# Row-vector broadcasts over 128 rows instead of 4, and the last modulation groups dealt between the late mixer steps

## Chip, core and metric

One Trainium2 chip, one core. The metric is the device time in microseconds of one execution of the whole program: 1726.24 us is the median of 3 runs of the kernel before (1725.05 to 1731.7).

## What is computed

One inference step of a recurrent decoder, two layers, all in fp32, on a prompt of 256 tokens and 8 sampled sequences of 8 tokens (320 token columns together). Cut to what matters here:

```python
mods = (silu(c) @ ada_w + ada_b).reshape(B, 3, 3, 1, D_MODEL)     # shift, scale, gate of three sublayers
x = residual(x, 0, swiglu(modulate(x, 0), ...), 0.5)
proj = modulate(x, 1) @ w_in
o_rw  = rwkv7_mix(p_rw, ...)      # 6 heads of 64
o_gla = gla_mix(p_gla, ...)       # 4 heads, keys of 48, values of 96
o_ml  = mlstm_mix(p_ml, ...)      # 4 heads of 64
mix = concatenate([o_rw, o_gla, o_ml]) @ w_out
x = residual(x, 1, mix, 1.0)
x = residual(x, 2, swiglu(modulate(x, 2), ...), 0.5)
```

Inside the mLSTM, three quantities are one number per head and token (a row vector of 320 elements for each of 4 heads): a weight of the carried state `w_inter`, the argument `b - m_t` of the decay matrix `Dw = exp(D - m_t)`, and `exp(-m_t)`, the floor of the denominator. Each must be spread over the 64 rows of its head before VectorE can multiply with it.

## The kernel before

The core works with the model dimension on the partitions and the 320 token columns along the free side. A weight tile of 128 x 1024 fp32 is loaded, split by ScalarE and VectorE into a high and a low part (`whi`, `wlo`), and each product takes three matmuls (lines 2017 to 2019). The order of all work is fixed ahead: `PLAN` is a list of steps, and the program of every engine walks through the same list, so each engine has its own piece of a step in the same place. Engines wait for each other through semaphores.

In each layer the plan is: up and down projections of the first feed-forward; the input projection; the three mixers; the output projection; the second feed-forward. The mixers are generators (`rw_pe`, `gl_pe`, `ml_pe` for TensorE, with ones for the other engines), and a step "rw", "gl" or "ml" runs one of them to its next `yield`:

- A first part, spread by `layer_plan`, in which the RWKV steps invert triangular matrices: batches of 64x64 matmuls (line 784), each followed by VectorE operations on their results (lines 1157 to 1172) that the next batch reads. I call it the inverse.
- A second part, whose order is the string `LATE` (line 99): the late steps. They hold the state recurrence of RWKV (lines 851 to 872, 900, 902), attention of GLA (1272, 1281, 1294, then 1315 to 1326 and the norm's 1334), and the mLSTM: `ml_pe` turns rows into columns (1535), spreads the row `E2` over both head pairs (1540, "pairsel"), for each of three token tiles spreads `ER` (1546, "headsel"), multiplies keys by queries (1555) and transposes (1562), builds the states (1573), spreads `D1` (1578), and then multiplies (1596, 1603, 1608); 1615 and 1620 are the norm. At the end the sampled states are advanced (1812, 914, 1821) and the first tiles of the output projection follow ("hi", "lo", "early").

`con("pairsel", P, rows=4, ...)` means that the weights of the spreading matmul are 4 rows by 128 columns, and the row vectors, tiles `IG` (also `E2`), `ER` and `D1`, have 4 partitions. They lie over the memory of `XH` and `XL`, the split inputs of the products. ScalarE zeroes rows 64 to 127 of the GLA part of `XH` and `XL` for the output projection (line 1368); that is one of its GLA steps.

The modulations `mods` are the filler. One group of them is four chunks: `ada` (line 2032) multiplies a 128 x 1024 tile of `ada_w` as the moving side, in four places of 32 output rows of a PSUM bank, `psC` or `psY`. The trace shows a chunk as 8 matmuls of 256 columns. After the fourth chunk ScalarE copies the bank to `MR` (line 2247, "mrow_done"), and a step `fold` (line 2042) on TensorE, which waits for that copy, turns it, and VectorE adds it to `MODS` (line 2344). `in_tail` lists the groups that are dealt into the inverse: 7 of them in layer 0 and 3 in layer 1. Their chunks are loaded through the ring `raw` of four buffers. The late steps hold no chunk.

The code that the change touches, with the line numbers of the profile:

## Time and profile before

| | us |
|---|---|
| median of 3 runs | 1726.24 |
| lowest and highest run | 1725.05, 1731.7 |
| the profiled execution | 1723.39 |
| its span, first to last instruction | 1721.4 |
| TensorE busy in it | 1645.3 (96%) |
| VectorE, ScalarE, GpSimd busy | 945.6, 663.3, 179.3 |
| mean granted clock of TensorE | 0.942 of full |

The profile is of one execution. "Busy" is the union of the intervals in which the engine has an instruction in it. PEclk is the share of its full clock that TensorE was granted: 1.00 is 2.4 GHz and 0.50 is 1.2 GHz. A line "L784 PE MATMUL psV<-Yb,Tt 64*64 64x64 f32 x24" is 24 matmuls of source line 784, whose weights are 64 rows by 64 columns and whose moving side is 64 rows of 64 columns. Bracketed at the end stands the idle time of the engine before the row and what ended it.

### The profile page before, as it was taken

The page shows a single profiled execution, that of the slowest core. Times are in us where ns is not written, and L with a number is a line of the kernel's source. Part 1 is how long each engine was busy: PE and PEld are TensorE (multiplying, and loading weights), DVE is VectorE, ACT ScalarE, POOL GpSimd, SP SyncE. Part 2 cuts the span into 40 slices and gives each one's busy share as a digit, 9 for nine tenths or more (in the row PEclk, how much of TensorE's full clock was granted, in tenths as well). Part 3 has the DMA queues.
Part 4 walks back from the last instruction along what each step waited for, and adds up shares of the span by engine and source line. Part 5 has one row for each costly group of instructions (what it writes and reads, how often), then busy time and mean ns, then how long its engine had stood idle before and what let it go on. Part 6 is the DMA issues. An engine that isn't in the chain of part 4 may idle for free.

```text
span 1721.4 us, 32986 instructions
## 1 busy us (share of the span) xinstructions
PE 1645.3 (96%) x14132; PEld 1517.5 (88%) x14132; DVE 945.6 (55%) x1605; ACT 663.3 (39%) x959; POOL 179.3 (10%) x247
## 2 busy tenths in 40 slices
PE   5999999999999999999999999999898999999997
PEld 2999998978778779999989999989877877899996
DVE  1544546584643776555474454467755457755544
ACT  2333334463323445333354333355432133543333
POOL 1000012100202140000110000110020123100011
PEclk9999999999975899999999999999997559999999
DMA  8765465433631174444765545643422104544441
GB/s 308 269 229 213 157 230 176 163 104 123 209 118 41 48 266 135 148 147 150 253 208 190 192 148 191 222 168 110 135 87 57 40 14 160 202 151 154 149 147 67
DMA packets 92512, 270.22 MB, mean 157 GB/s; under 512 B 27184, under 2 KB 29648, under 8 KB 92112
## 3 DMA queue, kind: packets, MB, share of 16 engines
q1 hardware_dynamic: 87952, 265.50, 45.0%
q10 hardware_dynamic: 4416, 2.62, 0.6%
q8 instruction: 112, 1.84, 0.5%
q14 instruction: 32, 0.26, 0.1%
HBM read 261.83 MB, written 6.26 MB: 156 GB/s over the span
## 4 chain that ended last, share of the span: by engine, by line
PE 82%; DVE 11%; DMA 3%; ACT 2%; issue 1%; SPq 0%; POOL 0%; DVEq 0%; ACTq 0%; POOLq 0%
PE psV L2017 12%; PE psV L2018 12%; PE psV L2019 12%; PE psA L2017 9%; PE psA L2019 9%; PE psA L2018 9%; PE psV L784 3%; DMA raw<-weights_dram 3%; DVE wlo L2335 2%; PE psY L2032 1%; PE psC L2032 1%; DVE PJ L1504 1%; PE psV L1608 1%; PE psV L773 1%; PE psV L2042 1%
## 5 line engine op out<-in xcount | busy, mean ns | idle before, releaser
L2335 DVE TENSOR_TENSOR wlo<-raw,whi 128x1024 fp32r<-128x1024 f32 x334 | 412.7, 1238 | 399.8 <-ACT whi L2193 397.2
L2193 ACT ACTIVATE whi<-raw 128x1024 fp32r<-128x1024 f32 x334 | 352.3, 1056 | 327.8 <-PE psV L2019 303.9
L2017 PE MATMUL psA<-XH,whi 128*128 128x320 f32 x1120 | 350.3, 313 | 12.1 <-DVE wlo L2335 10.4
L2018 PE MATMUL psA<-XL,whi 128*128 128x320 f32 x1120 | 347.6, 310 | 0.0
L2019 PE MATMUL psA<-XH,wlo 128*128 128x320 f32 x1120 | 347.4, 310 | 0.0
L2017 PE MATMUL psV<-XH,whi 128*128 128x320 f32 x848 | 267.1, 315 | 0.2
L2018 PE MATMUL psV<-XL,whi 128*128 128x320 f32 x848 | 264.1, 311 | 0.0
L2019 PE MATMUL psV<-XH,wlo 128*128 128x320 f32 x848 | 263.9, 311 | 0.0
L2017 PEld LDWEIGHTS psA<-XH,whi 128*128 128x128 f32 x1120 | 211.8, 189 | 16.1 <-issue 13.2
L2017 PE MATMUL psV<-HH,whi 128*128 128x320 f32 x704 | 217.5, 309 | 0.0
L2019 PE MATMUL psV<-HH,wlo 128*128 128x320 f32 x704 | 217.5, 309 | 0.0
L2018 PE MATMUL psV<-HL,whi 128*128 128x320 f32 x704 | 217.5, 309 | 0.0
L2018 PEld LDWEIGHTS psA<-XL,whi 128*128 128x128 f32 x1120 | 211.9, 189 | 0.3
L2019 PEld LDWEIGHTS psA<-XH,wlo 128*128 128x128 f32 x1120 | 211.8, 189 | 0.0
L2017 PEld LDWEIGHTS psV<-XH,whi 128*128 128x128 f32 x848 | 161.4, 190 | 7.3 <-issue 5.7
L2018 PEld LDWEIGHTS psV<-XL,whi 128*128 128x128 f32 x848 | 161.2, 190 | 0.6 <-issue 0.4
L2019 PEld LDWEIGHTS psV<-XH,wlo 128*128 128x128 f32 x848 | 161.1, 190 | 0.0
L2017 PEld LDWEIGHTS psV<-HH,whi 128*128 128x128 f32 x704 | 132.2, 188 | 0.0
L2018 PEld LDWEIGHTS psV<-HL,whi 128*128 128x128 f32 x704 | 132.2, 188 | 0.0
L2019 PEld LDWEIGHTS psV<-HH,wlo 128*128 128x128 f32 x704 | 132.2, 188 | 0.0
L2291 ACT ACTIVATE SG<-psA 128x320 f32<-128x320 f32 x84 | 36.7, 437 | 197.6 <-PE psA L2019 197.6
L2468 DVE TENSOR_TENSOR HF<-SG,psV 128x320 f32<-128x320 f32 x84 | 40.9, 487 | 91.8 <-PE psV L2019 91.8
(401 smaller groups left out, 1928.6 us busy)
## 6 DMA issues: line engine op xcount, KB each, us to landing
raw<-weights_dram SPq DMA_DIRECT2D x408, 512.0 KB, 3.3
own<-weights_dram SPq DMA_DIRECT2D x56, 512.0 KB, 6.1
in_xh<-weights_dram SPq DMA_DIRECT2D x6, 512.0 KB, 4.6
in_xl<-weights_dram SPq DMA_DIRECT2D x6, 512.0 KB, 4.7
raw<-weights_dram SPq DMA_DIRECT2D x8, 256.0 KB, 3.7
in_hl<-weights_dram SPq DMA_DIRECT2D x4, 512.0 KB, 5.4
ZS<-st_rw_dram SPq DMA_DIRECT2D x2, 768.0 KB, 4.3
S<-st_gla_dram ACTq DMA_DIRECT2D x2, 768.0 KB, 4.9
```

Of the source, the lines that this page charges most:

```text
L773: ins = mm(bank[c, o:o + 128].rearrange("p (x t) -> p x t", x=2), lhs[p, j, tc:tc + CH], AR[p, :, j, tc:tc + CH], start=True, stop=True)
L784: ins = mm(bank[c, h * CH:(h + 1) * CH], lhs, rhs, start=True, stop=True)
L1504: V.do(stt(out, x(tap), pcol("conv_w", 4 * tap + i), out, ALU.mult, ALU.add))
L1608: ins = mm(bank[p, SEQ + DS * s:SEQ + DS * (s + 1)], C0[p, j, s, part], QW[p, j, SEQ + DS * s:SEQ + DS * (s + 1)], start=False, stop=True, ...
L2017: mm(out, split_hi(n)[:, k], hi[:, kt], start=first, stop=False)
L2018: mm(out, split_hi(n)[:, k], lo[:, kt], start=False, stop=False)
L2019: return mm(out, split_lo(n)[:, k], hi[:, kt], start=False, stop=last)
L2032: ins = mm(psM[BANK[group]][o:o + 32, 0:256], CT[:, 2 * q + k], w[:, k, half], start=(q == 0), stop=(q == 3))
L2193: activation(split_hi(n), buffer(DENSE[n]), ACT.Copy).then_inc(hi_done, 1)
L2291: A.do(activation(SG[:, u % 2], bank[:, 0:TOK], ACT.Silu), sem("gate_done"))
L2335: tt(split_lo(n), buffer(DENSE[n]), split_hi(n).bitcast(F32), ALU.subtract).then_inc(lo_done, 1)
L2468: V.do(tt(HF[:, u % 2], SG[:, u % 2], bank[:, 0:TOK], ALU.mult), sem("hidden_done"))
```

## The change

Three edits that go together:

1. The spreading matmuls take all 128 rows of the constant (zeros in the rows from 4 on) and of the row tiles, which are now `[128, 320]`. Rows 4 to 127 of the tiles are zeroed first: one memset of `IG_all` on VectorE ahead of the mLSTM's first operations, and two, `ER_all` and `D1_all`, on GpSimd ahead of its mLSTM rows.
2. Since the tall tiles lie over the rows of `XH` and `XL` that ScalarE zeroes, that zeroing moves from the GLA step to the mLSTM step behind the last spreading.
3. The last 3 groups of `in_tail` in layer 0 and the last 2 in layer 1 (`IN_LATE`) leave the inverse. `LATE` has new places "ada" (both layers), "ada_" (layer 0 alone) and "fold" (layer 0 alone; other folds follow their chunk). Layer 0 gets 12 chunks in its late steps, layer 1 gets 8. All groups dealt late use the bank `psC`.

```diff
+LATE = ("rw ml ada gl rw ml ada gl ml ada_ rw gl ml ada rw gl ml ada ada_ gl ada rw ml ada_ gl ada rw ml ada gl ada_ ml ada rw fold "
+        "gl rw ml su mix rs rw rs su hi.0 rs lo.0 rw hi.1 rw hi.2 lo.1 early.0 rw lo.2 early.1 rw").split()
+IN_LATE = (3, 2)
...
-    out += spread([(step, 1) for step in together], ada_groups(in_tail))
+    out += spread([(step, 1) for step in together], ada_groups(in_tail[:-IN_LATE[L]]))
+    chunks = ada_groups(in_tail[-IN_LATE[L]:])
...
+        out.append(chunks.pop(0))
+        while chunks and chunks[0][0] == "fold":
+            out.append(chunks.pop(0))
...
-        BANK[_step[1:4]] = _b = GROUPS.index(_step[1:4]) % 2
+        BANK[_step[1:4]] = _b = 0 if _step[1:4] in LATE_GROUPS else GROUPS.index(_step[1:4]) % 2
...
+        IG_all, ER_all, D1_all = (over(f"row{i}_all", [P, TOK], at) for i, at in ((0, xh[3]), (4, xl[3]), (7, xl[6])))
+        IG, ER, D1 = IG_all[0:MH], ER_all[0:MH], D1_all[0:MH]
...
-                for x in (XH, XL):
-                    A.do(activation(x[64:P, RP:RP + GH], CON[64:P, 0:GH * TOK].rearrange("p (h t) -> p h t", t=TOK), ACT.Copy, scale=0.0))
-                A.mark(sem("gl_zero"))
...
-                    bV.close(mm(bank[:, 0:TOK], con("pairsel", P, rows=4, at=j * P), E2[:], start=True, stop=True))
+                    bV.close(mm(bank[:, 0:TOK], con("pairsel", P, at=j * P), IG_all[:], start=True, stop=True))
...
-                            ins = mm(bank[c, h * CH:(h + 1) * CH], con("headsel", CH, rows=4, at=h * CH), ER[:, tc:tc + CH],
+                            ins = mm(bank[c, h * CH:(h + 1) * CH], con("headsel", CH, at=h * CH), ER_all[:, tc:tc + CH],
...
-                    bA.close(mm(bank[:, 0:TOK], con("pairsel", P, rows=4, at=j * P), D1[:], start=True, stop=True))
+                    bA.close(mm(bank[:, 0:TOK], con("pairsel", P, at=j * P), D1_all[:], start=True, stop=True))
...
+                V.do(nc.vector.memset(IG_all[:], 0.0))
...
+                G.do(nc.gpsimd.memset(ER_all[:], 0.0))
+                G.do(nc.gpsimd.memset(D1_all[:], 0.0))
```

How the instructions move, at three places. The names: `psC<-raw,CT` and `psY<-raw,CT` are chunks (x4 here is one chunk, which the trace shows as 8), `psV<-FOLD,MR` a fold, `row_...,CON` a spreading.

TensorE in the inverse of layer 0, from the middle of a batch on, before:

```order
L784 MATMUL psV<-Tt_153,Yb_116 64x64 x6
L2032 MATMUL psC<-raw,CT 32x256 x4
L784 MATMUL psV<-Tn_111,AM_102 64x64 x12
L784 MATMUL psV<-Tn_112,AM_104 64x64 x12
L2032 MATMUL psY<-raw,CT 32x256 x8
L1264 MATMUL psA<-CON,PJ 128x128 x6
L1264 MATMUL psA<-CON,PJ 64x128 x3
L2042 MATMUL psV<-FOLD,MR 128x18 x2
L784 MATMUL psV<-Yb_114,Tt_151 64x64 x12
```

and with the change:

```order
L800 MATMUL psV<-Tt_153,Yb_116 64x64 x6
L2054 MATMUL psY<-raw,CT 32x256 x4
L800 MATMUL psV<-Tn_111,AM_102 64x64 x12
L800 MATMUL psV<-Tn_112,AM_104 64x64 x12
L2064 MATMUL psV<-FOLD,MR 128x18 x2
L1280 MATMUL psA<-CON,PJ 128x128 x6
L1280 MATMUL psA<-CON,PJ 64x128 x3
L2054 MATMUL psY<-raw,CT 32x256 x4
L800 MATMUL psV<-Yb_114,Tt_151 64x64 x12
```

Between the same batches stand fewer chunks: 16 in the whole part in place of 28.

TensorE at the first spreadings of the late steps of layer 0, before:

```order
L1540 MATMUL psV<-row_166,CON 128x320 x2
L1272 MATMUL psA<-CON,PJ 128x128 x2
L1281 MATMUL psV<-PJ,GB 64x64 x8
L868 MATMUL psV<-U_122,TK_101 64x64 x6
L872 MATMUL psV<-TK_101 64x64 x6
L1546 MATMUL psV<-row_170,CON 64x64 x8
L1555 MATMUL psV<-PJ 64x64 x8
L1562 MATMUL psV<-CON,PJ 128x128 x2
L1272 MATMUL psA<-CON,PJ 128x128 x2
```

and with the change:

```order
L1553 MATMUL psV<-row_all,CON 128x320 x2
L2054 MATMUL psC<-raw,CT 32x256 x4
L1288 MATMUL psA<-CON,PJ 128x128 x2
L1297 MATMUL psV<-PJ,GB 64x64 x8
L884 MATMUL psV<-U_122,TK_101 64x64 x6
L888 MATMUL psV<-TK_101 64x64 x6
L1559 MATMUL psV<-row_all,CON 64x64 x8
L1568 MATMUL psV<-PJ 64x64 x8
L1575 MATMUL psV<-CON,PJ 128x128 x2
L2054 MATMUL psC<-raw,CT 32x256 x4
L1288 MATMUL psA<-CON,PJ 128x128 x2
```

A chunk now follows the first spreading and each token tile. In the later steps one follows each GLA product (1326) and, in layer 0, each mLSTM product (1608).

TensorE at the norms, near the end of the late steps of layer 0, before:

```order
L1334 MATMUL psV<-PJ,CON 96x320 x4
L1615 MATMUL psV<-PJ,CON 128x320 x2
L868 MATMUL psV<-U_123,TK_103 64x64 x6
L872 MATMUL psV<-TK_103 64x64 x6
L851 MATMUL psV<-Z,WT_149 64x64 x6
```

with the change:

```order
L1350 MATMUL psV<-PJ,CON 96x320 x4
L2054 MATMUL psC<-raw,CT 32x256 x4
L1628 MATMUL psV<-PJ,CON 128x320 x2
L2054 MATMUL psC<-raw,CT 32x256 x4
L2064 MATMUL psV<-FOLD,MR 128x18 x2
L884 MATMUL psV<-U_123,TK_103 64x64 x6
L888 MATMUL psV<-TK_103 64x64 x6
```

and ScalarE at the same place, with the change:

```order
L1399 ACTIVATE PJ<-PJ 96x1280
L1676 ACTIVATE PJ<-PJ 128x640
L2269 ACTIVATE MR<-psC 128x256
L1680 ACTIVATE PJ<-psV,EPS 128x320 x2
```

The last fold of the layer follows its own last chunk at once, and the copy to `MR` for which it waits stands in ScalarE's row behind the square of the mLSTM's output (line 1660 before, 1676 now).

## Rows read from the trace of the kernel before

**Rows 1.** The page: span, TensorE's share, and its granted clock in 40 slices

```profile
span 1721.4 us, 32986 instructions
...
PE 1645.3 (96%) x14132; PEld 1517.5 (88%) x14132; DVE 945.6 (55%) x1605; ACT 663.3 (39%) x959; POOL 179.3 (10%) x247
...
PEclk9999999999975899999999999999997559999999
```

**Rows 2.** Windows in us: length, busy time (instructions) of each engine, granted clock, DMA

```profile
445.00:483.70 38.70, 38.45 (x953) 32.42 (x953) 26.79 (x55) 10.34 (x19) 6.88 (x14) 1.00 0.64 215
501.60:522.00 20.40, 20.02 (x249) 16.42 (x244) 10.33 (x34) 4.43 (x7) 0.00 (x0) 0.50 0.15 32
...
525.50:559.60 34.10, 33.63 (x451) 30.40 (x448) 10.48 (x17) 9.19 (x14) 11.19 (x7) 0.50 0.07 29
...
1272.80:1311.20 38.40, 36.14 (x866) 32.03 (x865) 28.08 (x53) 9.88 (x16) 7.60 (x15) 0.91 0.24 80
1313.90:1324.20 10.30, 10.16 (x161) 8.85 (x157) 0.00 (x0) 5.45 (x13) 0.00 (x0) 0.50 0.01 2
...
1327.60:1351.00 23.40, 22.95 (x270) 18.50 (x270) 11.73 (x39) 4.82 (x8) 0.00 (x0) 0.50 0.17 45
1351.00:1392.40 41.40, 40.26 (x472) 34.34 (x472) 13.07 (x25) 13.19 (x18) 12.47 (x8) 0.50 0.11 40
```

**Rows 3.** Timeline, TensorE: start, length, what (rows*columns of the weights, moving side)

```profile
499.09 1.32 PE L1540 MATMUL psV<-row,CON 4*128 4x320 f32 x4
...
502.85 1.11 PE L1546 MATMUL psV<-row,CON 4*64 4x64 f32 x16
...
555.88 4.21 PE L1334 MATMUL psV<-PJ,CON 96*96 96x320 f32 x8
```

**Rows 4.** Timeline, TensorE: like work at full and at half clock

```profile
1279.91 0.92 PE L784 MATMUL psV<-Yb,Tt 64*64 64x64 f32 x24
...
1298.07 1.49 PE L784 MATMUL psV<-Tt,Yb 64*64 64x64 f32 x24
...
494.96 2.48 PE L831 MATMUL psA<-RB,Tt 64*64 64x64 f32 x60
...
1319.29 1.08 PE L2032 MATMUL psY<-raw,CT 128*32 128x256 f32 x8
1320.30 4.05 PE L831 MATMUL psA<-RB,Tt 64*64 64x64 f32 x60
```

**Rows 5.** Chain of waits, inverse of layer 1: a chunk, a fold, the copy to MR

```profile
1276.61 0.57 PE psC L2032 x8
...
1284.32 0.55 PE psV L2042 x4
...
1293.36 0.38 ACT MR L2247
```

**Rows 6.** Timeline, TensorE in the inverse of layer 1: its longest wait

```profile
1296.33 0.52 PE L1264 MATMUL psA<-CON,PJ 128*64 128x128 f32 x3 [2.24 <-ACT VG L1352]
```

**Rows 7.** Timeline, layer 0: VectorE, GpSimd and ScalarE near the added and moved operations

```profile
440.03 1.28 DVE L1142 TENSOR_TENSOR AM<-psV,CON 64x512 f32<-64x512 f32 x2 [3.08 <-PE psV L773]
...
455.36 0.85 POOL L1779 TENSOR_TENSOR LF<-LF,row 4x320 f32<-4x320 f32 x1 [10.45 <-ACT row L1639]
456.17 0.44 POOL L1780 COPY row<-row 4x320 f32<-4x320 f32 x1
...
516.82 1.27 ACT L1368 ACTIVATE XH<-CON 64x1280 fp32r<-64x1280 f32 x1
```

**Rows 8.** Timeline, layer 0, at the norms

```profile
560.67 1.03 DVE L1754 TENSOR_TENSOR PJ<-PJ,psV 128x320 f32<-128x320 f32 x2 [3.22 <-PE psV L1615]
...
561.86 0.72 ACT L1660 ACTIVATE PJ<-PJ 128x640 f32<-128x640 f32 x1
562.07 0.36 DVE L1189 TENSOR_TENSOR Z<-psV,ZP 128x192 f32<-128x192 f32 x1 [0.37 <-PE psV L872]
...
566.73 2.74 PE L1812 MATMUL psV<-VG,KX 64*64 64x96 f32 x61 [1.84 <-DVE U L1184]
```

More of the change, by code:

```diff
@@ L96 @@
 GL_FIRST, ML_FIRST = 3, 4
-LATE = ("rw ml gl rw ml gl ml rw gl ml rw gl ml gl rw ml gl rw ml gl ml rw gl rw ml su mix rs rw rs su hi.0 rs lo.0 rw "
-        "hi.1 rw hi.2 lo.1 early.0 rw lo.2 early.1 rw").split()
+LATE = ("rw ml ada gl rw ml ada gl ml ada_ rw gl ml ada rw gl ml ada ada_ gl ada rw ml ada_ gl ada rw ml ada gl ada_ ml ada rw fold "
+        "gl rw ml su mix rs rw rs su hi.0 rs lo.0 rw hi.1 rw hi.2 lo.1 early.0 rw lo.2 early.1 rw").split()
+IN_LATE = (3, 2)
 EARLY_FIRST = 5
@@ L201, in layer_plan @@
     together = spread([(rw[0], int(k > 1)) for k in range(RW_INVERSE)], first)
-    out += spread([(step, 1) for step in together], ada_groups(in_tail))
-    out += [(name.split(".")[0], L, *map(int, name.split(".")[1:])) for name in LATE]
+    out += spread([(step, 1) for step in together], ada_groups(in_tail[:-IN_LATE[L]]))
+    chunks = ada_groups(in_tail[-IN_LATE[L]:])
+    for name in LATE:
+        if name == "fold" or name == "ada_" and IN_LATE[L] < 3:
+            continue
+        if name not in ("ada", "ada_"):
+            out.append((name.split(".")[0], L, *map(int, name.split(".")[1:])))
+            continue
+        out.append(chunks.pop(0))
+        while chunks and chunks[0][0] == "fold":
+            out.append(chunks.pop(0))
+    assert not chunks
     steps, left = product(("out", L), 1, in_gaps[1])
@@ L324 @@
     _last[SLOT[_n]] = _n
+LATE_GROUPS = set()
+for _L in range(DEPTH):
+    _groups = [step[1:4] for step in PLAN[:PLAN.index(("rs", _L))] if step[0] == "ada" and step[4] == 0]
+    LATE_GROUPS.update(_groups[-IN_LATE[_L]:])
 BANK, EARLIER, _in = {}, {}, {}
@@ L594, in hybrid_trunk @@
         GT = over("GT", [P, RP, NS], xl[2])
-        IG, FZ, BM, MM, ER, CR, D0, D1 = (over(f"row{i}", [MH, TOK], at)
-                                          for i, at in enumerate(xh[3:7] + xl[3:7]))
+        FZ, BM, MM, CR, D0 = (over(f"row{i}", [MH, TOK], (xh[3:7] + xl[3:7])[i]) for i in (1, 2, 3, 5, 6))
+        IG_all, ER_all, D1_all = (over(f"row{i}_all", [P, TOK], at) for i, at in ((0, xh[3]), (4, xl[3]), (7, xl[6])))
+        IG, ER, D1 = IG_all[0:MH], ER_all[0:MH], D1_all[0:MH]
         LF, E2, WJ = over("LF", [MH, TOK], xl[2]), IG, FZ
@@ L1655, in ml_act @@
                 A.mark(sem("ml_emb"))
+                for x in (XH, XL):
+                    A.do(activation(x[64:P, RP:RP + GH], CON[64:P, 0:GH * TOK].rearrange("p (h t) -> p h t", t=TOK), ACT.Copy, scale=0.0))
+                A.mark(sem("gl_zero"))
                 A.do(activation(PJ[:, T_MO:T_MO + MP], PJ[:, T_MO:T_MO + MP], ACT.Sigmoid), sem("ml_gate"))
@@ L1672, in ml_vec @@
                 V.mark(sem("ml_start"))
+                V.do(nc.vector.memset(IG_all[:], 0.0))
+                V.settle()
                 V.do(ts(IG[:], PJ[32:36, T_LOW], pcol("i_b", 0, 32, 36), None, ALU.add))
@@ L1776, in c64 @@
                     return ap.rearrange("p (c t) -> p c t", t=CH)
+                pool.wait_ge(*at("ml_f", 1))
+                G.do(nc.gpsimd.memset(ER_all[:], 0.0))
+                G.do(nc.gpsimd.memset(D1_all[:], 0.0))
+                G.settle()
                 pool.wait_ge(*at("ml_log", 1))
```

## The prediction

> **What bounds the kernel now.** I read the page first. TensorE is busy for 1645.3 of the 1721.4 us, and nearly every slice of its row reads 9: it is the bound almost everywhere [rows 1]. A change of this kind can pay only by making TensorE's own work shorter or by filling its waits. The row PEclk shows where there is something to get: it is 9 throughout except for slices 12 to 14 and 31 to 34, where it falls to 5 [rows 1]. Both are the late steps of a mixer.
>
> The windows view puts edges on these places [rows 2]. In layer 0 the granted clock is 0.50 from 501.6 to 522.0 us and again from 525.5 to 559.6. In layer 1 it is 0.50 from 1313.9 to 1324.2, from 1327.6 to 1351.0 and from 1351.0 to 1392.4. (I cut the last stretch at 1351.0 because there the first kind of work ends.) This is 1.2 GHz in place of 2.4. In all of them TensorE is busy: 20.02 of 20.40 us, 33.63 of 34.10, 40.26 of 41.40. It does not wait for anybody, it is slow. VectorE is busy only 10.33 of 20.40 and 10.48 of 34.10 us there. So time taken from TensorE in these stretches is time taken from the kernel, until VectorE's chains show.
>
> What was TensorE doing when the clock fell? At 499.09 to 500.4 it ran the first spreading, 4 rows of weights by 128 columns [rows 3], and at 501.6 the clock was down. Then come spreadings with weights of 4 rows by 64 columns [rows 3], 64x64 products, and products of 8 columns. It rose again at 559.6, behind the norm's matmuls of 96x96 weights and 320 columns, which started at 555.88 [rows 3]. In the inverse of layer 0, with chunks of 128 rows between the 64x64 batches, it stayed at 1.00 for all of 38.70 us [rows 2]. So the trace goes with the idea that what the matmuls fill of the array matters, and not only that one is running.
>
> **Part 1: the clock in the late steps.** What is a microsecond at half clock worth? Like work at both levels [rows 4]: 24 matmuls of line 784 take 0.92 and 1.49 us, 60 of line 831 take 2.48 and 4.05. That is 0.62 and 0.61 of the time at full clock, so I take 0.6: each microsecond that goes from half to full saves 0.4.
>
> I split the low time in two. The first kind (20.4 + 23.4 = 43.8 us) is from the first spreading to the states. All spreading matmuls in it become 128 rows tall, and a chunk follows the first of them and nearly every token tile. I take all of it as recovered: 43.8 x 0.4 = 17.5 us saved. The second kind (34.1 + 41.4 = 75.5 us) holds no spreading but the last one, at its edge; its long runs (lines 1596, 1603, 1608, 1326) stay as thin as they are and get one chunk each in layer 0, and in layer 1 a chunk behind each GLA product, but none between the first mLSTM product and the second GLA one. A chunk every 5 us or more is much less than in the inverse. I take half: 37.75 x 0.4 = 15.1 us. Together 32.6 us. For the bounds: nothing of either, or all of both, 119.3 x 0.4 = 47.7. The 10.3 us at 1313.9 lie ahead of the spreadings and lose a chunk, and the stretches behind the last fold get none; I leave them as they are.
>
> The Trainium skill's page "TensorE: Matmul & The Clock Gate" says in its section "Why this matters for your kernels" that throughput drops mid-kernel are avoided by leaving no idle gaps between bursts of matmuls, and its Part 1 says that the clock follows how busy the engine has been. By that rule an engine that is already busy is not helped by taller weights, and part 1 would be 0 and not 32.6 us; the third rival follows from it.
>
> **Part 2: the taller spreadings themselves.** They stream as many columns as before. The nearest rows are the 4-row matmuls of 320 columns, 1.32 us for four, against the 96-row ones of 320 columns, which took 4.21 us for eight at half clock [rows 3], 2.5 us at the 0.6 above, or 1.26 for four. So 0, with 0.1 us each way.
>
> **Part 3: the memsets and the moved zeroing.** The nearest row to a memset of 320 elements on GpSimd is its copy of 4x320, 0.44 us [rows 7]; twice that stands before an operation for which GpSimd waited 10.45 us [rows 7]. Cost 0; without that cover 0.9. VectorE's one memset, about 0.5 by the same row, stands ahead of operations in front of which it idled 3.08 us [rows 7]; without that cover it is 0.5 per layer. ScalarE's two zeroings, 1.27 us each [rows 7], now stand ahead of a table load, the gate's sigmoid and the copies of the first GLA product. TensorE has a chunk and the whole GLA product to do until those copies are due, so 0 again; if not, about 1 us per layer.
>
> **Part 4: chunks leave the inverse.** 12 chunks and 3 folds in layer 0, 8 and 2 in layer 1: 20 x 0.57 + 5 x 0.55 = 14.2 us of TensorE's time [rows 5], moved, not removed. At full clock it is paid again in the late steps. The question is whether the inverse gives it back. Layer 1 is the measurement: its inverse has 7 chunks between the first and the last batch where layer 0 has 17, and it takes 38.40 us against 38.70 [rows 2]. Ten chunks less and nothing gained: TensorE waited 2.24 us for ScalarE in one place [rows 6], and the granted clock was 0.91 there against 1.00 [rows 2]. The other bound is that all 14.2 come back. In the late steps, on the other hand, the chunks fill waits that the full clock would open (VectorE's 10.33 us would lie in some 14). I take half, 7 us lost.
>
> **Part 5: the last fold.** It waits for its own chunk's copy to `MR`. That copy stands behind line 1660 on ScalarE, which squares what VectorE makes in line 1754. In the trace 1660 ends at 561.86 + 0.72 = 562.58 [rows 8]; then 0.38 for the copy and 0.55 for the fold [rows 5] give 563.5, and only then come the 24 matmuls of 64x64 (868, 872) that VectorE needs for Z, 0.92 by the row of as many [rows 4], so Z comes at 564.4 in place of 562.07. Behind that Z, VectorE works up to U, for which TensorE already waits 1.84 us at 566.73 [rows 8]. So the delay of 2.4 us is on the path, and in layer 1 the fold also brings four small operations on VectorE, some 0.8 us. Sum 2.4 + 3.2 = 5.6, say 5.5 us lost. Bounds: 0, if the norms come so early that ScalarE is ahead, and 8.
>
> **The sum.** -32.6 + 7 + 5.5 = -20.1, say -20 us. The profiled execution took 1723.39 us (span 1721.4), so it would take 1703.3. The median, 1726.24, lies 2.85 above it; the forecast of the median is **1706 us**. Its own range is 1696 to 1714.
>
> **The rivals.**
>
> 1. *The full clock holds in all late steps.* For: once at full clock, two batches fall into the time of one, which helps it stay there, and a full clock held through the inverse of layer 0. Against: the 8-column products are very thin. -47.7 + 12.5 = -35, so 1691.
> 2. *It holds in the first kind only.* A product of line 1608 follows and it falls at once, to rise where it rises now. For: layer 1 has no chunk there. -17.5 + 12.5 = -5, so 1721.
> 3. *The clock stays low*, because it follows being busy, as the page says, or because a chunk is too little. Price: 20 chunks at half clock cost 1.08 each [rows 4] and the folds some 0.9, 26 us in the late steps, against half of 14.2 back from the inverse, and the fold's wait shrinks to perhaps 2: +21, so 1747. This one ends on the other side. It decides against the change when less than some 30 us (12.5 / 0.4) of the low time is recovered. Against it: TensorE was as busy in the inverse of layer 0, 38.45 of 38.70, as in the slow stretches.
> 4. *The low clock moves forward.* With 12 and 8 chunks less, TensorE waits more in the inverse and falls there, as it did twice in layer 1. At 20 us of new low time in each layer +16 on the forecast: 1722.
>
> **How the numbers follow.** 0.5% of the time, 8.6 us, is about what a measurement of this kernel can tell from no change: faster means below 1717.6, slower above 1734.9. The forecast has 0.45, rival 1 0.20, rival 2 0.15, rival 3 0.09, rival 4 0.11. The forecast and rival 1 are faster, with a third of 2 and 4 by the width of their costs: 0.74. The rest of 2 and 4 is the same, 0.16, and with the tail of the lost terms slower is 0.10. The range takes in rival 1 with its costs a little smaller and rivals 2 and 4, and leaves out rival 3: **1686 to 1725**.
>
> **What would show it.** The spreading rows keep their length at full clock. In the windows view the stretch from the first spreading to the states stands at 1.00, and the second stretch is mixed; each microsecond at 0.50 that is gone shows as 0.4 us less. The inverse of layer 0 gets shorter by less than its 12 chunks, with rows of waiting TensorE in it, and a fold waits for `MR` behind the norms. The prediction is wrong if the late steps stay at 0.50 with chunks among them, if the inverse falls to 0.50 for long, or if the late steps at full clock show TensorE waiting on VectorE for more than a few microseconds.

## The result, and the profile after

| | before | changed |
|---|---|---|
| median, lowest and highest of 9 runs each, us | 1725.05 (1716.81 to 1733.54) | 1711.15 (1705.04 to 1718.12) |
| profiled execution, span, us | 1721.4 | 1711.5 |

The ratio is 0.9918 with a 95% interval of [0.9892, 0.9945]: faster by 0.8%, 14 us. The forecast was 20 us. The total is near; not all of its terms are.

The page of the changed kernel, the lines that answer to [rows 1]:

```profile
span 1711.5 us, 32995 instructions
...
PE 1634.3 (95%) x14132; PEld 1502.8 (88%) x14132; DVE 945.5 (55%) x1607; ACT 663.8 (39%) x959; POOL 180.9 (11%) x251
...
PEclk9999999999986799999999999999998769999999
```

The low digits of PEclk are higher than before, and they are still there. To see which work gained I cut both mixers at the same five places: the inverse (from its first 64x64 batch), the products of lines 813, 823 and 831 behind it, the first kind of late work (from the first row transposed by line 1535 to the spreading of `D1`), the second stretch (from there to the first matmul of line 1812), and the closing stretch up to the output projection. The windows view of the kernel before, with the columns of [rows 2], the first four stretches of layer 0 and then of layer 1:

```profile
445.00:487.50 42.50, 39.01 (x959) 32.50 (x955) 29.87 (x62) 10.82 (x19) 6.88 (x14) 1.00 0.65 223
487.50:498.80 11.30, 11.16 (x229) 9.90 (x229) 1.75 (x7) 5.86 (x14) 0.00 (x0) 0.85 0.01 2
498.80:522.40 23.60, 23.15 (x279) 18.49 (x278) 12.29 (x44) 4.82 (x8) 0.00 (x0) 0.57 0.23 58
522.40:566.70 44.30, 40.73 (x526) 35.05 (x525) 18.52 (x36) 15.78 (x22) 12.47 (x8) 0.61 0.11 39
...
1272.80:1312.90 40.10, 36.14 (x866) 32.03 (x865) 29.64 (x56) 9.88 (x16) 7.60 (x15) 0.91 0.23 77
1312.90:1325.70 12.80, 12.63 (x217) 11.16 (x217) 1.58 (x6) 5.94 (x14) 0.00 (x0) 0.60 0.01 1
1325.70:1350.80 25.10, 24.57 (x280) 19.17 (x279) 13.36 (x48) 4.82 (x8) 0.00 (x0) 0.54 0.22 57
1350.80:1398.30 47.50, 43.91 (x528) 36.86 (x527) 18.27 (x36) 15.89 (x22) 12.47 (x8) 0.56 0.10 35
```

The same of the changed kernel, and last its closing stretch of layer 1:

```profile
443.70:484.40 40.70, 38.26 (x891) 33.15 (x887) 29.52 (x60) 9.27 (x16) 7.44 (x16) 0.92 0.38 130
484.40:497.10 12.70, 12.56 (x216) 11.09 (x216) 1.55 (x5) 5.95 (x14) 0.00 (x0) 0.60 0.17 54
497.10:516.80 19.70, 18.95 (x314) 12.87 (x311) 12.35 (x44) 2.78 (x7) 0.00 (x0) 1.00 0.57 175
516.80:566.30 49.50, 45.45 (x602) 34.34 (x601) 19.30 (x40) 18.98 (x26) 12.48 (x8) 0.69 0.26 89
...
1275.50:1309.50 34.00, 30.24 (x826) 27.39 (x825) 28.82 (x54) 8.88 (x15) 8.28 (x17) 1.00 0.15 49
1309.50:1321.70 12.20, 12.04 (x208) 11.52 (x208) 1.68 (x6) 5.69 (x13) 0.00 (x0) 0.58 0.01 3
1321.70:1340.50 18.80, 18.31 (x306) 12.71 (x303) 12.27 (x44) 2.40 (x6) 0.00 (x0) 1.00 0.50 155
1340.50:1391.80 51.30, 47.99 (x574) 37.78 (x573) 21.05 (x42) 17.50 (x25) 12.60 (x8) 0.58 0.17 55
1391.80:1414.50 22.70, 20.28 (x297) 17.22 (x298) 16.23 (x27) 8.55 (x13) 5.33 (x4) 0.75 0.07 25
```

- The first kind went from 0.57 and 0.54 of the clock to 1.00 in both layers, and from 23.6 and 25.1 us to 19.7 and 18.8, with four chunks more in it in layer 0 and three in layer 1.
- The second stretch did not follow: 0.61 to 0.69 in layer 0 and 0.56 to 0.58 in layer 1. With its share of chunks it grew from 44.3 to 49.5 and from 47.5 to 51.3 us.
- The inverse gave back 1.8 us in layer 0 and 6.1 in layer 1.

A stretch of length t with mean clock c has had 2 x (1 - c) x t us at half clock. For the second stretch of both layers this is 34.6 + 41.8 = 76 us before and 30.7 + 43.1 = 74 after. I call it the half-clock time.

The added operations, by the timeline. TensorE's new and taller matmuls in layer 0, and the three places of the changed kernel where it waits for the new copies to `MR`:

```profile
497.50 1.34 PE L1553 MATMUL psV<-row_all,CON 128*128 128x320 f32 x4
498.78 0.64 PE L2054 MATMUL psC<-raw,CT 128*32 128x256 f32 x8
501.31 0.69 PE L1559 MATMUL psV<-row_all,CON 128*64 128x64 f32 x16
...
560.16 0.62 PE L2064 MATMUL psV<-FOLD,MR 128*128 128x18 f32 x4 [1.11 <-ACT MR L2269]
...
1347.32 1.08 PE L2054 MATMUL psC<-raw,CT 128*32 128x256 f32 x8 [0.82 <-ACT MR L2269]
...
1385.23 0.62 PE L2064 MATMUL psV<-FOLD,MR 128*128 128x18 f32 x4 [1.11 <-ACT MR L2269]
```

The spreading of 320 columns takes 1.34 us for four with 128 rows where it took 1.32 with 4 [rows 3]. So height is free at 320 columns. That of 64 columns went from 1.11 us for sixteen at half clock to 0.69 at full; the same sixteen with 4 rows at full clock are in e6_pairsel_only below. The last fold waits 1.11 us in each layer, and one chunk waits 0.82: all late groups share `psC`, and the next group can't start until its predecessor is copied out. VectorE's memset took 0.33 us and GpSimd's four 0.36 each, and ScalarE's two zeroings (1.27 and 1.25 us) stood behind 5.06 us of waiting, and 0.24 us of waiting for TensorE followed them. None of them made TensorE wait.

### The profile page after: what moved, and what is told of

Its sections match the earlier page's. It is cut to its first block, busy times and chain, and to the rows that moved or that the text cites. A ratio compares the mean times of both kernels' runs of the same rounds, so it can differ in the third digit from the quotient of the medians.

```text
span 1711.5 us, 32995 instructions
## 1 busy us (share of the span) xinstructions
PE 1634.3 (95%) x14132; PEld 1502.8 (88%) x14132; DVE 945.5 (55%) x1607; ACT 663.8 (39%) x959; POOL 180.9 (11%) x251
## 3 DMA queue, kind: packets, MB, share of 16 engines
q8 instruction: 112, 1.84, 0.4%
## 4 chain that ended last, share of the span: by engine, by line
PE 82%; DVE 10%; DMA 4%; ACT 2%; issue 1%; SPq 0%; POOL 0%; DVEq 0%; ACTq 0%; POOLq 0%
PE psV L2039 12%; PE psV L2040 12%; PE psV L2041 12%; PE psA L2039 9%; PE psA L2041 9%; PE psA L2040 9%; DMA raw<-weights_dram 4%; PE psV L800 3%; DVE wlo L2357 2%; PE psC L2054 2%; PE psY L2054 1%; DVE PJ L1517 1%; PE psV L2064 1%; ACT whi L2215 1%; PE psV L1621 1%
```

## The experiments

Three questions were open: which of the three edits holds the gain, why the second stretch stayed low, and whether the chunks earn anything. All twelve runs, below the two kernels, come first as one table, made with the windows view at the same five places. Each cell is the length in us, with the mean granted clock in brackets; L0 and L1 are the layers.

| kernel | span | L0 inverse | products | first kind | second | closing | L1 inverse | products | first kind | second | closing |
|---|---|---|---|---|---|---|---|---|---|---|---|
| before | 1721.4 | 42.5 (1.00) | 11.3 (0.85) | 23.6 (0.57) | 44.3 (0.61) | 22.0 (0.69) | 40.1 (0.91) | 12.8 (0.60) | 25.1 (0.54) | 47.5 (0.56) | 26.4 (0.55) |
| changed | 1711.5 | 40.7 (0.92) | 12.7 (0.60) | 19.7 (1.00) | 49.5 (0.69) | 26.5 (0.55) | 34.0 (1.00) | 12.2 (0.58) | 18.8 (1.00) | 51.3 (0.58) | 22.7 (0.75) |
| e0_again | 1699.0 | 39.1 (0.96) | 11.4 (0.70) | 19.7 (1.00) | 39.7 (0.87) | 23.8 (0.64) | 34.0 (1.00) | 12.2 (0.58) | 18.7 (1.00) | 51.5 (0.58) | 27.2 (0.53) |
| e11_after | 1717.2 | 39.1 (0.96) | 9.7 (1.00) | 19.7 (1.00) | 53.0 (0.60) | 27.3 (0.53) | 37.8 (0.87) | 8.8 (1.00) | 18.7 (1.00) | 51.7 (0.59) | 27.3 (0.53) |
| e1_tall_only | 1702.6 | 43.1 (1.00) | 11.3 (0.85) | 17.6 (0.97) | 42.6 (0.65) | 26.5 (0.55) | 40.1 (0.91) | 10.8 (0.84) | 17.5 (1.00) | 40.1 (0.70) | 26.4 (0.55) |
| e12_tall | 1709.5 | 42.7 (0.99) | 15.0 (0.56) | 17.2 (1.00) | 41.5 (0.67) | 26.4 (0.55) | 40.1 (0.91) | 13.8 (0.55) | 19.2 (0.88) | 42.9 (0.64) | 26.5 (0.55) |
| e2_moves_only | 1724.2 | 37.7 (1.00) | 12.7 (0.60) | 28.9 (0.59) | 51.5 (0.63) | 27.9 (0.51) | 34.0 (1.00) | 8.8 (1.00) | 19.8 (0.86) | 54.3 (0.53) | 27.2 (0.53) |
| e3_first_kind | 1707.6 | 43.1 (0.94) | 11.7 (0.74) | 19.6 (1.00) | 39.8 (0.70) | 28.0 (0.52) | 35.1 (1.00) | 12.0 (0.57) | 19.3 (1.00) | 47.2 (0.57) | 26.5 (0.55) |
| e5_held | 1704.9 | 39.1 (0.96) | 9.8 (1.00) | 19.6 (1.00) | 53.2 (0.84) | 26.4 (0.55) | 34.1 (1.00) | 8.7 (1.00) | 18.8 (1.00) | 45.7 (0.96) | 26.5 (0.55) |
| e6_pairsel_only | 1718.9 | 42.7 (1.00) | 13.9 (0.63) | 17.6 (0.90) | 47.0 (0.57) | 26.5 (0.55) | 40.2 (0.92) | 13.7 (0.55) | 19.6 (0.76) | 45.5 (0.60) | 26.4 (0.55) |
| e7_rows64 | 1700.2 | 39.0 (0.96) | 11.6 (0.71) | 18.4 (1.00) | 50.9 (0.63) | 22.3 (0.69) | 36.6 (0.91) | 8.8 (1.00) | 17.9 (0.98) | 49.4 (0.60) | 22.7 (0.75) |
| e8_dense | 1702.2 | 35.0 (1.00) | 12.1 (0.58) | 17.3 (1.00) | 52.6 (0.84) | 26.5 (0.55) | 34.0 (1.00) | 12.3 (0.58) | 17.3 (0.99) | 46.3 (0.71) | 26.5 (0.55) |
| e9_ahead | 1696.4 | 43.7 (0.95) | 10.1 (1.00) | 17.2 (1.00) | 41.4 (0.67) | 26.5 (0.55) | 35.1 (1.00) | 8.8 (1.00) | 17.2 (1.00) | 39.8 (0.70) | 28.0 (0.51) |
| e10_inside | 1700.8 | 35.2 (1.00) | 8.8 (1.00) | 17.4 (1.00) | 45.6 (0.89) | 28.0 (0.51) | 34.0 (1.00) | 8.8 (1.00) | 17.3 (0.99) | 54.2 (0.59) | 28.1 (0.51) |

A span here is of one execution. The verdicts below go by the medians and the ratios to the kernel before, which was run on the same chip each time (medians 1725.77, 1729.05 and 1727.97 us for the three sets).

One execution is little to go by, but every execution on record has its mean granted clock. By the same formula over the whole span, the mean half-clock time of an execution is 212 us for the kernel before (51 executions), 161 for the changed one (19), 157 with the tall spreadings alone (16), 189 with the moved chunks alone (10), 143 in e9_ahead (6) and 127 in e5_held (10).

### The changed kernel again: e0_again and e11_after

No edit; they stand beside the others of their sets.

> The changed kernel, unaltered, on the chip of the next three. Its profiled execution was 9.9 us shorter than the one before: the stretches from the first spreading to the states lost their half clock and 4.0 and 6.4 us, the stretches behind them kept theirs (30.7 and 43.1 us at half clock) and grew by 5.3 and 3.8 us. If the falls of the clock follow the program, the same stretches are at half clock again and their lengths repeat within 1 us. If they are chance, the pattern changes and so do the lengths; the closing stretches of the mixers, which the change does not touch, differed by 4 us in both directions and are the first suspects. About 1711 us.

> The changed kernel once more, so that tall spreadings alone can be set beside it on one chip. The two measurements so far gave ratios of 0.9918 and 0.9886 to the kernel before, so 0.990, some 1709 us. If the chunks in the late steps earn what they cost, it stands level with e12_tall within 3 us; if they cost more than they earn, e12_tall is faster by 5 us or more.

Measured: e0_again 1703.57 us (4 runs), ratio 0.9886 [0.9838, 0.9935]; e11_after 1710.78 us (6 runs), 0.9907 [0.9874, 0.994]. With the first result that is three times about 0.99. Their rows in the table show how far one program differs between executions: the second stretch of layer 0 was 39.7, 49.5 and 53.0 us at 0.87, 0.69 and 0.60, with the same instructions in the same order. A single profile of such a stretch proves little. The first kind was at 1.00 in all six cases.

### The tall spreadings alone: e1_tall_only and e12_tall

Edits 1 and 2 stay, edit 3 is undone (`LATE` and the chunks as before).

```diff
-    out += spread([(step, 1) for step in together], ada_groups(in_tail[:-IN_LATE[L]]))
-    chunks = ada_groups(in_tail[-IN_LATE[L]:])
...
+    out += spread([(step, 1) for step in together], ada_groups(in_tail))
+    out += [(name.split(".")[0], L, *map(int, name.split(".")[1:])) for name in LATE]
```

> The spreadings over 128 rows alone, all chunks in the inverse as before. If tall spreadings hold the clock in the first stretch by themselves, it shrinks from 23.7 and 25.1 us to about 17 and 16 (it holds no chunk), everything else stays as before, and the time is some 12 us under before, 1713. If the chunks held it, the first stretch stays at half clock at about 24 us and the time is that of before, 1725.

> Tall spreadings alone, all chunks in the inverse, once more. Theory A (the tall spreadings are the whole gain): 0.989, level with e11_after. Theory B (the chunks in the late steps hold the clock in the second stretch and are worth a few us): slower than e11_after by 3 us or more.

Measured: 1706.74 us (10 runs), 0.9899 [0.9868, 0.993]; again 1709.45 us (6 runs), 0.99 [0.9867, 0.9932]. The first is 3 us above the changed kernel of its set, the second 1 us below that of its own: level, within the 5 to 6 us that such few runs can tell. **No gain is left for the chunks: the tall spreadings have all that can be told.** The windows view of e1_tall_only, first kind and second stretch, layer 0 and layer 1:

```profile
500.50:518.10 17.60, 17.11 (x280) 12.92 (x279) 12.46 (x45) 2.39 (x6) 0.00 (x0) 0.97 0.31 81
518.10:560.70 42.60, 39.04 (x526) 32.32 (x525) 18.28 (x36) 18.20 (x24) 12.47 (x8) 0.65 0.12 40
...
1321.80:1339.30 17.50, 17.01 (x282) 12.62 (x279) 12.99 (x47) 2.39 (x6) 0.00 (x0) 1.00 0.30 78
1339.30:1379.40 40.10, 36.51 (x528) 30.23 (x527) 18.56 (x36) 18.20 (x24) 12.47 (x8) 0.70 0.12 44
```

With as many matmuls as before (280 and 279, 282 and 280) the first kind takes 6.0 and 7.6 us less. The second stretch gains too, 1.7 and 7.4 us, with its clock at 0.65 and 0.70. It is one profile against one.

### The moves alone: e2_moves_only

Edits 2 and 3 stay; the spreadings take 4 rows again.

```diff
-                    bV.close(mm(bank[:, 0:TOK], con("pairsel", P, at=j * P), IG_all[:], start=True, stop=True))
+                    bV.close(mm(bank[:, 0:TOK], con("pairsel", P, rows=4, at=j * P), E2[:], start=True, stop=True))
```

and so for "headsel" and `D1`.

> The moved chunks alone, with spreadings of 4 rows by the same tiles. If chunks alone hold the clock, the first stretch is at full clock, 19 to 20 us, and the time is that of the change, 1711. If the tall spreadings do it, the first stretch is at half clock with three or four chunks in it, some 27 us, the inverse is shorter as in the change, and the time is 1720 to 1730.

Measured: 1722.17 us (10 runs), 0.9977 [0.9944, 1.001]. No change that can be told. This kernel differs from the changed one in nothing but the rows of the spreadings, and it is 18.6 us slower than e0_again in the same set. That is the direct test of the first edit. Windows, first kind and second stretch in each layer:

```profile
493.10:522.00 28.90, 28.17 (x313) 18.80 (x311) 12.36 (x44) 2.78 (x7) 0.00 (x0) 0.59 0.40 119
522.00:573.50 51.50, 48.43 (x604) 36.75 (x602) 19.32 (x40) 18.16 (x25) 12.47 (x8) 0.63 0.26 85
...
1327.10:1346.90 19.80, 19.36 (x305) 14.50 (x302) 12.61 (x45) 2.39 (x6) 0.00 (x0) 0.86 0.50 147
1346.90:1401.20 54.30, 51.76 (x574) 40.39 (x572) 20.77 (x42) 17.60 (x24) 12.59 (x8) 0.53 0.16 52
```

A chunk behind nearly every token tile doesn't hold the clock by itself: 0.59 in layer 0, 0.86 in layer 1. What the inverse gives back here (42.5 to 37.7 us and 40.1 to 34.0) the late steps take again. The effects of the two halves, 0.9899 and 0.9977, multiplied give 0.9876, against 0.9918, 0.9886 and 0.9907 measured together, so they don't help each other.

### Chunks in the first kind only: e3_first_kind

One group per layer is dealt late, all of it among the spreadings, and its fold three steps behind its last chunk. The rest stays in the inverse.

```diff
-IN_LATE = (3, 2)
+IN_LATE = (1, 1)
...
+"rw ml ada gl rw ml ada gl ml ada rw gl ml ada rw gl ml fold gl rw ml gl ..."
```

> Tall spreadings; only one group per layer (4 chunks) goes late, behind the first spreading and the three token tiles, its fold behind the last spreading; the second stretch holds no chunk. If chunks in the second stretch are paid there in full (they were: 49.6 and 51.3 us with them, 42.6 and 40.1 without), this gives first stretches of 19.7 us, second ones of some 40 to 43, an inverse 2 us shorter in both layers than with all chunks, and no wait of a fold behind the norms: 1700 to 1705 us, a few under the change. If the chunks in the second stretch help it at all, it is slower than the change by what they helped.

Measured: 1706.85 us (4 runs), 0.9881 [0.9846, 0.9917]. Level with the tall spreadings alone. Four chunks cost the first kind some 2 us (19.6 and 19.3 against 17.2 to 17.6 at full clock); layer 1's inverse gave 5 back, and its second stretch (47.2 at 0.57) took it.

### Half the height: e7_rows64

The changed kernel, chunks included, with 64 rows in place of 128.

```diff
-con("pairsel", P, at=j * P), IG_all[:]
+con("pairsel", P, rows=64, at=j * P), IG_all[0:64]
```

and so for the other two.

> The change with spreadings of 64 rows in place of 128. If how much of the array the spreadings fill decides, and 4 rows were far too few, half the height may still hold the clock with the chunks beside it: first stretches of 19.7 us, 1704 to 1711 us. If it takes the full height, the first stretch is at half clock for most of its length, 27 us, and the time is that of the moved chunks alone, 1722.

Measured: 1712.75 us (10 runs), 0.9908 [0.9878, 0.9939], as with 128 rows. The first kind stood at 1.00 and 0.98. So 64 rows of zeros and weights do what 128 do, with the chunks beside them; without chunks they were not tried.

### Tall for two of the three: e6_pairsel_only

All chunks in the inverse; "pairsel" (for `E2` and `D1`) takes 128 rows, "headsel" 4 as before.

```diff
-                            ins = mm(bank[c, h * CH:(h + 1) * CH], con("headsel", CH, at=h * CH), ER_all[:, tc:tc + CH],
+                            ins = mm(bank[c, h * CH:(h + 1) * CH], con("headsel", CH, rows=4, at=h * CH), ER[:, tc:tc + CH],
```

> Tall spreadings without the moved chunks, but only the ones of 320 columns (pairsel, 4 of them per layer); those of 64 columns (headsel) stay at 4 rows. If the fall at the first spreading starts it all, the clock is held there, and the first stretch keeps most of its gain: 18 to 19 us in place of 17.6, 1707 us. If the headsel ones are needed, the clock falls behind the first spreading again and the stretch is 22 to 24 us, 1717 us or more.

Measured: 1713.37 us (6 runs), 0.9912 [0.9876, 0.9948]. The median can't tell it from e1_tall_only. Its first kind can:

```profile
502.10:519.70 17.60, 17.16 (x279) 13.71 (x279) 12.49 (x45) 2.39 (x6) 0.00 (x0) 0.90 0.32 81
...
1330.70:1350.30 19.60, 19.15 (x279) 15.24 (x278) 12.96 (x46) 2.39 (x6) 0.00 (x0) 0.76 0.25 68
```

0.90 and 0.76, against 0.57 and 0.54 with no tall spreading and 0.88 to 1.00 with all of them. Inside this stretch only the spreading of `E2` is tall, four matmuls as the trace shows them; that of `D1` stands at its end. So these four carry the larger part of the effect, and the forty "headsel" ones the rest. How much that is, one profile can't say. This run also has the short spreading at full clock, with 4 rows of weights:

```profile
505.56 0.68 PE L1544 MATMUL psV<-row_all,CON 4*64 4x64 f32 x16
```

0.68 us, as with 128 rows (0.69): height is free at 64 columns too.

### Holding the clock by force: e5_held

The changed kernel, with extra matmuls in the second stretch: weights of 128 x 128 constants against 320 or 192 constant columns, at places ahead of and between lines 1326, 1596 and 1608. They write bank space that is overwritten or never read, so they add work and no result.

```diff
+            def extra(banks):
+                for bank in banks:
+                    nc.tensor.matmul(bank[:, 0:TOK], con("ones64", P), con("level", TOK), start=True, stop=True)
...
+                    extra(banks)
...
+                        for n in range(2):
+                            mm(bank[:, TOK:512], con("ones64", P), con("level", 512 - TOK), start=False, stop=True, skip_group_check=True)
```

> The change, with matmuls of 128 rows by 128 columns that nobody reads put among the thin products of the second stretch (into the banks ahead of each accumulation and between the 64x64 and the 8-column products): per layer 8 of 320 columns and 8 of 192, some 3.5 us at full clock. The theory that the thin products let the clock fall expects the second stretch at full clock in both layers and its length to go from 49.6 and 51.3 us to 0.6 of it plus 3.5, 33 to 36, so 1711 - 30 = 1681 us, or less gain where VectorE or ScalarE is then waited for. The rival that the clock falls there whatever is added expects 49.6 + 6 us at half clock and 1723 us.

Measured: 1716.28 us (10 runs), 0.995 [0.9916, 0.9984]. The windows of its second stretches:

```profile
512.10:565.30 53.20, 49.14 (x634) 34.68 (x633) 19.30 (x40) 18.97 (x26) 12.47 (x8) 0.84 0.24 82
...
1336.10:1381.80 45.70, 41.11 (x606) 30.18 (x605) 21.89 (x42) 18.75 (x26) 12.59 (x8) 0.96 0.19 61
```

and two pairs of the extra matmuls in layer 1, each of which the trace shows as four:

```profile
1338.06 1.32 PE L1534 MATMUL psA<-CON 128*128 128x320 f32 x4
...
1350.69 0.92 PE L1625 MATMUL psV<-CON 128*128 128x192 f32 x4
```

The clock is held: 0.96 in layer 1 where the changed kernel has 0.58, 0.58 and 0.59, and over all ten executions the half-clock time is 127 us and not 161. In layer 0 the 0.84 is inside what the changed kernel reaches by itself (0.60 to 0.87). So the second stretch was low because of what its matmuls were, and adding matmuls with full weights and many columns raises the clock; which of the two does it was not tried apart. But such a row of four moves what follows by some 1.27 us with 320 columns and by 0.85 with 192. There are four rows of each per layer, 8.5 us at full clock, where I had expected 3.5. Layer 1 fell from 51.5 us (mean of three) to 45.7 with that in it; without it the 39 us of half clock that are gone gave back 14.3 us, 0.36 each. Matmuls that nobody needs cost more here than they give: by the medians this kernel is 12.7 us slower than e0_again.

### Many chunks, close together: e8_dense and e10_inside

e8_dense deals five groups late in layer 0 and two in layer 1, none in the first kind, three chunks in a row in the second stretch of layer 0:

```diff
-IN_LATE = (3, 2)
+IN_LATE = (5, 2)
...
+"... ml ada ada ada gl ada ada ada rw ml ada ada ada gl ada ada ada rw ml ada ada ada gl ada ada ada ml ada ada rw gl rw fold ml ..."
```

> Tall spreadings; 5 groups in layer 0 and 2 in layer 1 go late, all of them into the second stretch, two or three chunks in a row in layer 0. If dense chunks hold the clock, layer 0's second stretch is at full clock with 20 chunks in it, some 30 + 11.4 = 41 us, its inverse is 6 us shorter than with all chunks, and the time is 1695 to 1700. If the thin products inside one step let it fall all the same, the stretch takes 50 us and more (42.6 + 20 x 0.57 to 1.0), and the time is 1710 to 1715.

Measured: 1704.28 us (4 runs), 0.9875 [0.9833, 0.9918]. With 20 chunks layer 0's second stretch stood at 0.84; it took 52.6 us, and the inverse gave back 7.5 (42.5 to 35.0). VectorE was busy for 27.42 us there instead of 19.30, and DMA moved 202 GB/s instead of 89.

e10_inside deals four and two groups, all into the second stretch; new `yield`s inside the mLSTM's step put chunks within the runs of lines 1596 to 1608, and the last fold stands behind the next RWKV step. Some of the inverse's chunks stand ahead of the products of line 813, where TensorE waits:

```diff
-IN_LATE = (3, 2)
+IN_LATE = (4, 2)
...
+                yield
...
+"... rw ml ada ada ml ada ada gl ada ml ada rw gl rw fold ml su ..."
```

> Tall spreadings, the late chunks all behind the spreading of D1 (none in the first kind of work, where tall spreadings suffice), with some inside the thin runs of lines 1596 to 1608, and the last fold behind the next RWKV step so that it doesn't wait for its copy to MR. Theory A (tall weights close together hold the clock in the second stretch): half-clock time in it falls from 30 to 43 us per layer to under 15, the fold's wait of 1.1 us goes, 6 to 12 us under e11_after, some 1700 us. Theory B (single chunks never hold the clock over the thin runs): half-clock time stays over 25 us per layer and the time is level with e11_after.

Measured: 1705.29 us (6 runs), 0.9884 [0.9837, 0.993]; e11_after in the same set 1710.78. A gain of 6 to 12 us was expected; 5.5 came, with runs from 1697 to 1717 us, so it can't be told from none. In layer 0 the half-clock time fell to 10 us (0.89), as the first theory said; in layer 1, with half as many chunks, it was 44 us (0.59), as the second said. Its last folds start without a wait. Its products stood at 1.00 in both layers. The number of chunks would fit this, 16 late ones in layer 0 and 8 in layer 1, and the 0.84 of e8_dense with 20. It isn't shown: with 8 chunks in layer 0 the changed kernel stood at 0.87 in one of its three profiles, and with 8 in layer 1 e8_dense stood at 0.71. By the medians neither kernel can be told from the tall spreadings alone.

### Chunks where TensorE waits: e9_ahead

Tall spreadings, no chunk in the late steps, but the inverse's chunks are not spread evenly: one place, ahead of the products of line 813, takes more of them, three in a row in layer 0 and two behind a fold in layer 1. The others move a little.

```diff
-    out += spread([(step, 1) for step in together], ada_groups(in_tail))
+    ahead = [i for i, step in enumerate(together) if step == rw[0]][-2] - 1
+    weight = [(3, 6)[L] if i == ahead else 1 for i in range(len(together))]
+    out += spread(list(zip(together, weight)), ada_groups(in_tail))
```

> Tall spreadings, all chunks in the inverse, but three of them in each layer placed ahead of the 64x64 products of lines 813 to 831, where TensorE waits 2 to 3 us for VectorE. Theory A (a chunk costs nothing where TensorE waits, and tall weights there keep the clock through these products): the stretch of 10.8 to 12.8 us falls to some 9 us in both layers, the inverse shrinks by 1 to 2 us, in all 3 to 6 us under e12_tall. Theory B (falls of the clock at that place come of themselves): the stretch keeps its half clock and the kernel is level with e12_tall.

Measured: 1700.44 us (6 runs), 0.9845 [0.9812, 0.9878]. **The fastest of all**: 9 us under e12_tall and 10 under the changed kernel in the same set, six runs each; their scatter leaves these differences uncertain by some 6 us. TensorE at the products of layer 1, in e12_tall:

```profile
1311.23 0.85 PE L814 MATMUL psA<-TK,AM 64*64 64x64 f32 x21 [1.74 <-DVE Tt L1173]
...
1313.22 1.21 PE L814 MATMUL psA<-TK,AM 64*64 64x64 f32 x18
```

and in e9_ahead:

```profile
1305.53 1.07 PE L2041 MATMUL psY<-raw,CT 128*32 128x256 f32 x16
1306.79 0.85 PE L816 MATMUL psA<-TK,AM 64*64 64x64 f32 x21 [0.19 <-DVE Tt L1175]
...
1308.52 0.69 PE L816 MATMUL psA<-TK,AM 64*64 64x64 f32 x18
```

Two chunks fill the wait for VectorE, 1.74 us becomes 0.19, and 18 of the products behind take 0.69 us instead of 1.21. The windows of inverse and products in layer 1 of e9_ahead:

```profile
1271.70:1306.80 35.10, 34.15 (x879) 29.44 (x875) 27.93 (x54) 11.95 (x19) 7.33 (x16) 1.00 0.28 93
1306.80:1315.60 8.80, 8.23 (x209) 7.52 (x209) 2.60 (x10) 5.68 (x14) 0.00 (x0) 1.00 0.01 2
```

Before they took 40.1 and 12.8 us, with 4.0 us of waiting in the inverse where now 0.95 are left. By the profiles, layer 1's inverse and products are 10 us shorter than in e12_tall and layer 0's 4 us. I had expected 3 to 6 in all, since I took the inverse for nearly full. Of layer 1's 10 us, 1.55 are the wait at line 814 and 2.0 are a wait for ScalarE inside the inverse (2.24 us at line 1265 in e12_tall, 0.25 here), which went as the other chunks moved; in layer 0 that same wait came up, from 0.25 to 2.24. The rest is clock: 19.6 us of half clock are gone. One profile with the products at 1.00 in both layers would be weak, as e11_after and e5_held had that too. But e10_inside has chunks at the same place and the same clock, so with the wait filled the products stood at 1.00 in four stretches of four, and without them, in the twelve other profiles, in 6 of 24. That and the medians carry it.

## Why the prediction was right, and which of its steps was not

**What bounds the kernel: right.** TensorE is busy and slow in the late steps, and the time came from its clock.

**Part 1, the first kind: mechanism right, price off.** All of it was recovered, by the spreadings alone. At full clock and without chunks it takes 17.2 (e12_tall) and 17.5 us (e1_tall_only) against 23.6 and 25.1: 14.0 us for 43 us of half clock, 0.32 each and not 0.4. Over whole executions the same comes out: the tall spreadings alone have 55 us less at half clock and are 18 us shorter, 0.33 each, and among executions of one kernel the time goes with the half-clock time by some 0.31 (an estimate, the slope over all executions with a clock on record). The 0.4 came from 64x64 matmuls [rows 4]. Others lose less. TensorE's groups of instructions by line in the first kind of layer 1, before at 0.50:

```profile
L1555 PE MATMUL psV<-PJ 64*64 64x64 f32 x40 | 4.1, 324 | 0.2
...
L1573 PE MATMUL psV<-VM,KW 64*64 64x128 f32 x32 | 3.0, 429 | 0.0
```

and the same lines in e9_ahead at 1.00:

```profile
L1555 PE MATMUL psV<-PJ 64*64 64x64 f32 x40 | 2.7, 230 | 0.2
L1573 PE MATMUL psV<-VM,KW 64*64 64x128 f32 x32 | 2.5, 281 | 0.0
```

2.7 of 4.1 us is 0.66, 2.5 of 3.0 is 0.83.

**Part 1, the second kind: this step failed.** "I take half" of 75.5 us, 15.1 us saved. The changed kernel went from 76 us at half clock to 74 (71 as the mean of its three profiles), worth 2 us. I had argued with the chunks, and single chunks 5 us apart do little here: in layer 1 the stretch stood at 0.58, 0.58 and 0.59, in layer 0 at 0.69, 0.87 and 0.60. The spreadings alone brought both layers to 56 us (mean of e1_tall_only and e12_tall). A start at full clock isn't the reason. The spreading of `D1` heads the stretch, and its length, 1.34 or 2.50 us, tells the level; in layer 0 of the kernel before, in layer 0 of e1_tall_only and in layer 1 of the changed kernel it is

```profile
522.42 1.34 PE L1578 MATMUL psA<-row,CON 4*128 4x320 f32 x4
...
518.09 2.50 PE L1576 MATMUL psA<-row_all,CON 128*128 128x320 f32 x4
...
1340.48 1.34 PE L1591 MATMUL psA<-row_all,CON 128*128 128x320 f32 x4
```

The first starts at full clock and has 34.6 us at half, the second starts at half and has 29.8, the third starts at full, falls some 5 us later and has 43.1. What lowered the half-clock time there stays open, and so does how much of it is chance between executions. The step had no row under it: no stretch of the trace showed single chunks among thin matmuls, and the inverse of layer 1, at 0.91 with only seven chunks [rows 2], was a sign that the count of chunks doesn't settle the clock. In the changed kernel it stands at 1.00 with three, and the products behind it, 64x64 too and nearly without waits, at 0.58. Why these two differ stays open.

**Part 2 and part 3, cost 0: right**, by the rows of the changed kernel above.

**Part 4, half of 14.2 us comes back: right for the inverse.** It gave back 7.9 us in the profile of the changed kernel and 8.1 in the mean of its three against tall spreadings alone, more of it in layer 1. What was missing is the price at the other end. Put the three profiles of the changed kernel beside the two with tall spreadings alone: inverse -8.1 us, products -3.1, first kind +2.7, second stretch +15.4, closing -1.3, the rest -2.3. The sum is +3. The second stretch pays 1.08 us for a chunk at half clock [rows 4], which I had charged at 0.57, and is left with more half-clock time than without chunks. The excess is all in layer 1, 42.9 us against 27.5 (in layer 0 it is 27.8 against 28.6). There, in the profile of the changed kernel, three chunks and a fold ran at half clock, 4.3 us in sum, and the clock, up again at the norms, was down again for the last 4 us in all three profiles, where it stays up in both profiles with tall spreadings alone. The rest stays open, and it may be chance: e3_first_kind, with no chunk in that stretch, had 40.6 us at half clock, and over whole executions the two kernels differ by 4 us only (161 and 157).

**Part 5, the last fold: mechanism right, size off.** 2.4 and 3.2 us were forecast. The fold waits 1.11 us in each layer and moves what follows by 0.55, so 1.7 us each and 3.3 together; the extra VectorE operation on `MODS` takes 0.20 us. Behind the fold the chain in layer 0 is as written: the 24 matmuls, Z, a wait of 0.55 us, U, a wait of 1.83 where it was 1.84, so the delay is on the path. A wait that I had not seen is that of a chunk for its bank, 0.82 us.

**The sum.** The first kind gave 14 instead of 17.5 and the second 2 instead of 15; the fold took 3.3 instead of 5.5. Things that I had not priced stand on either side: the chunks at half clock and a closing stretch that is 3.2 us longer in the mean of the three profiles (against), the products with 1.8 us and all that lies outside the five stretches with 2.7 (for). That the total came within 6 us is partly luck. One reading was off by a slice: the low digits of PEclk in layer 1 are slices 31 to 33, not 31 to 34; nothing hangs on it, since the edges came from the windows.

**The rivals.** Rival 2, first kind only, was nearest to what happened: the first kind is what recovered, and it came to 1721 for the changed kernel through the two costs that proved smaller. Rival 1 falls with the second stretch. Rival 4 shows in part: layer 0's inverse, at 1.00 before, has 3 to 7 us at half clock in the three profiles of the changed kernel, but layer 1's lost its 7 us in two of them. Rival 3 is refuted: in the kernel before, TensorE was busy for 24.57 of 25.10 us at 0.54, and in the changed one it was busy for 30.24 of 34.00 at 1.00. The less busy engine had the higher clock.

The Trainium skill's page "TensorE: Matmul & The Clock Gate", Part 1 and the section "Why this matters for your kernels", has the clock follow the engine's activity in time. Where a gap was filled, in e9_ahead and e10_inside, the trace agrees: four stretches of four at 1.00. With no gap to fill, the measurement decides against it: the first kind of layer 1 was busy for 24.57 of 25.10 us at 0.54 with 4 rows and for 17.01 of 17.50 at 1.00 with 128.

## What to carry to other kernels

Where the granted clock is low and the engine is busy, look at how much of the array the matmuls fill: here selector matmuls with 4 rows took zeros up to 64 or 128 rows at no cost in time, and at 128 rows that alone brought back the clock of their stretch. Filler work earns its place where the engine waits, ahead of a chain of another engine; in a stretch at half clock it cost nearly double (1.08 us a chunk for 0.57), and single chunks showed no gain; dense ones kept the clock up in the profiles, but the medians show no gain from them either. A stretch whose clock differs between executions is judged by medians of runs of each part of the change, since one profile can show the change's effect in either direction.
